# Where the four early heads are scaled in a head loop: one item sooner in VectorE's order

## What is computed

```python
def diff_core(q, k, v, q_pos, k_pos, lam):
    s = jnp.einsum('bqhjd,bkhjd->bhjqk', q, k, preferred_element_type=jnp.float32) * (DIFF_HEAD_DIM ** -0.5)
    mask = k_pos[None, :] <= q_pos[:, None]
    s = jnp.where(mask[None, None, None], s, NEG_INF)
    p = jax.nn.softmax(s, axis=-1)
    a = p[:, :, 0] - lam * p[:, :, 1]
    return jnp.einsum('bhqk,bkhe->bqhe', a.astype(v.dtype), v)
...
            o = rmsnorm(o, p['subln'][j]) * (1.0 - lam_init)
            mix = o.reshape(B, T, MIX_WIDTH)
        x = x + jnp.concatenate([mix, mem_out], axis=-1) @ p['w_out'][l]
```

## Time and profile before

| | |
|---|---|
| Median of 3 runs | 1242.99 us (1237.56, 1242.99, 1243.36) |
| The profiled execution | 1243.28 us |
| Its span | 1241.4 us |
| Mean granted clock of TensorE | 0.985 |
| TensorE busy | 1176.9 us (95%) |
| VectorE busy | 852.2 us (69%) |
| ScalarE busy | 508.5 us (41%) |
| POOL busy | 451.2 us (36%) |

### The profile page before, as it was taken

One profiled execution on the slowest core, in us unless ns is written; L12 is line 12 of the kernel. 1 busy time (PEld: TensorE's weight loads), 2 busy tenths in 40 slices (PEclk: granted clock), 3 DMA queues, 4 the chain that ended last, 5 costly groups with the idle time before them and its releaser, 6 DMA issues.

```text
span 1241.4 us, 23819 instructions
## 1 busy us (share of the span) xinstructions
PE 1176.9 (95%) x9342; PEld 1125.0 (91%) x9342; DVE 852.2 (69%) x1316; ACT 508.5 (41%) x962; POOL 451.2 (36%) x348
## 2 busy tenths in 40 slices
PE   5999898999999999999999988898999999999996
PEld 5878898999999999999899855798999999999996
DVE  6767688776776767656543787569777767767634
ACT  6545444444333433334422266434534334333321
POOL 3354035453444444212037111014544434444302
PEclk9999999999999999999999999799999999999998
DMA  7632421323223223423254277022223232232212
GB/s 273 224 128 60 142 86 52 129 76 104 101 69 119 86 73 116 148 73 102 86 157 126 87 259 258 11 86 69 86 88 116 69 116 88 69 119 86 88 49 72
DMA packets 46228, 134.95 MB, mean 109 GB/s; under 512 B 4178, under 2 KB 6354, under 8 KB 45490
## 3 DMA queue, kind: packets, MB, share of 16 engines
q1 hardware_dynamic: 45026, 125.39, 30.2%
q0 software_dynamic: 1104, 8.15, 2.2%
HBM read 123.15 MB, written 7.03 MB: 105 GB/s over the span
## 4 chain that ended last, share of the span: by engine, by line
PE 74%; DVE 12%; POOL 5%; DMA 3%; issue 3%; ACT 3%; SPq 0%; DVEq 0%; ACTq 0%; POOLq 0%
PE psum L647 29%; PE psum L629 22%; PE psum L563 15%; DVE weights_split L1420 2%; PE psum L813 1%; DVE inv_rms L1441 1%; PE psum L997 1%; DMA rotated<-projected 1%; POOL projected L2118 1%; POOL projected L2119 1%; ACT weights_split L1042 1%; DMA rotated<-keys 1%; PE psum L718 1%; DMA weights_raw<-in_weights 1%; POOL rotated L2117 1%
## 5 line engine op out<-in xcount | busy, mean ns | idle before, releaser
L647 PE MATMUL psum<-operand_b,weights_split 128*128 128x272 f32 x1536 | 197.1, 290 | 3.7 <-DVE weights_split L1509 1.9
L647 PEld LDWEIGHTS psum<-operand_b,weights_split 128*128 128x128 f32 x1536 | 195.1, 190 | 4.3 <-DVE weights_split L1509 2.2
L647 PE MATMUL psum<-operand_a,weights_split 128*128 128x272 f32 (+1 forms) x1536 | 195.3, 288 | 3.3 <-DVE weights_split L1509 1.9
L647 PEld LDWEIGHTS psum<-operand_a,weights_split 128*128 128x128 f32 x1536 | 193.5, 188 | 3.7 <-DVE weights_split L1509 2.2
L563 PE MATMUL psum<-operand_b,weights_split 128*128 128x272 f32 x1344 | 176.0, 291 | 4.4 <-DVE weights_split L1420 4.2
L563 PEld LDWEIGHTS psum<-operand_b,weights_split 128*128 128x128 f32 x1344 | 171.1, 190 | 9.3 <-DVE weights_split L1420 5.2
L563 PE MATMUL psum<-operand_a,weights_split 128*128 128x272 f32 (+1 forms) x948 | 126.7, 292 | 17.9 <-DVE weights_split L1420 13.9
L563 PEld LDWEIGHTS psum<-operand_a,weights_split 128*128 128x128 f32 x948 | 121.0, 192 | 23.9 <-issue 17.5
L1042 ACT ACTIVATE weights_split<-weights_raw 128x1024 fp32r<-128x1024 f32 (+1 forms) x66 | 66.5, 1008 | 134.2 <-PE psum L563 125.6
L1989 POOL TENSOR_TENSOR mem_keys<-weights_raw 128x512 f32<-128x512 f32 x28 | 36.7, 1312 | 219.3 <-DMA weights_raw<-in_weights 219.3
L1420 DVE TENSOR_TENSOR weights_split<-weights_raw,weights_split 128x1024 fp32r<-128x1024 f32 (+1 forms) x66 | 90.7, 1377 | 16.2 <-ACT weights_split L1042 16.1
(11 more groups left out here) (286 smaller groups left out, 2086.0 us busy)
## 6 DMA issues: line engine op xcount, KB each, us to landing
weights_raw<-in_weights SPq DMA_DIRECT2D x186, 512.0 KB, 3.7
cache_tiles<-in_page_k SPq DMA_DIRECT2D x16, 384.0 KB, 4.0
cache_tiles<-in_page_v SPq DMA_DIRECT2D x16, 384.0 KB, 4.3
cache_tiles<-in_mem_k SPq DMA_DIRECT2D x8, 512.0 KB, 4.6
cache_tiles<-in_mem_v SPq DMA_DIRECT2D x8, 512.0 KB, 5.1
residual<-in_x SPq DMA_DIRECT2D x1, 2176.0 KB, 12.0
rotated<-projected POOLq DMA_DIRECT2D x4, 408.0 KB, 7.0
rotated<-keys POOLq DMA_DIRECT2D x4, 408.0 KB, 7.1
```

Of the source, the lines that this page charges most:

```text
L647: mm = pe.matmul(ps[:, bank, 0:part.stop - part.start], w(wr), hidden[:, ar, 4 * (c % 2) + kk, part], start=(kk == 0 and wr == 0 and ar == 0),
```

## The change

The wait for sub_rms and the four scales are placed in step EARLY_DONE + 3 = 44 of VectorE's loop and no longer in step 45. There they stand behind weight(44), drain(42) and bias(46), and ahead of weight(45), drain(43) and bias(47). Nothing else is changed.

```diff
@@ -1712,7 +1712,7 @@
                     if n == EARLY_DONE + 1:
                         dve.wait_ge(squared, EARLY)
                         means(ss[:, 0:EARLY], 0, EARLY)
-                    if n == EARLY_DONE + 4:
+                    if n == EARLY_DONE + 3:
                         dve.wait_ge(sub_rms, 1)
                         for h in range(EARLY_HEADS):
                             scale_head(h)
```

## The result

The changed kernel takes 1233.68 us (median of nine runs, 1232.68 to 1238.57), the kernel before 1241.38 us in the same set (nine runs, 1237.56 to 1243.36). The ratio is 0.9945, with a 95% interval of 0.9929 to 0.9961: 0.55% faster, some 7 us. The profiled execution took 1233.68 us, its span is 1231.8.

The account below looks back on a forecast made before the run. TensorE, busy 95% of the span, was taken as the bound, waiting on VectorE's path through the scales to turn(46). Median 1242.99 less 1.3 us, clock unchanged, gave 1241.7 us; range 1236.3 to 1243.9.

Parts of the forecast that it names:

- Step 1: VectorE's scales behind bias(46): POOL's sub_rms is ready at 777.77, VectorE free at 777.96, so no wait, margin 0.19 us.
- Step 2: VectorE's order from 777.96: the scales fill its 1.38 us hole, so turn(46) starts at 784.30 instead of 785.68.
- Step 3: What becomes late: turn(45) by 1.3 us, hidden with 0.8 in hand; exp(47) by 1.02; turn(47) still gains some 1.28.
- Step 4: From turn(47) on TensorE is nearly full and transfers quiet, so everything moves up together; gain 1.3 us.
- 1.3 us: Gain on VectorE's path to turn(46) and turn(47), taken between 1.28 and 1.38 us.
- 0.06 us for POOL's clamp: First scale behind bias(46) might be held by POOL's clamp until 778.02, 0.06 later, making the gain 1.24 us.
- the term for the clock: TensorE's clock ahead of turn(46): about as thinly used after the change, so expected to fall as now; no gain counted.
- the base of 1242.99: Median of three earlier runs of the kernel before, from which the forecast subtracted its gain to reach 1241.7 us.
- Rival B: TensorE's clock never falls because its pieces lie closer together; at most 6.2 us, about 1236.5 us; chance 0.07.
- Rival A: TensorE's clock is back one step earlier because dense matmuls L997 start sooner; 1.7 us more, 1240.0 us; chance 0.25.
- C: No gain: VectorE's hole is replaced by another of the same length; 1243.0 us; chance 0.11.
- D: Slower: POOL's chain to sub_rms is late and VectorE stands in front of weight(45); 1244.4 us; chance 0.05.

Follow-up runs that it names:

- the filled kernel before: The kernel before plus eight useless TensorE matmuls, four ahead of and four behind the transposes of heads 0 and 1; 1237.85 us, ratio 0.9970.
- the pair of four matmuls: The kernel before plus four useless matmuls only ahead of the transposes of heads 0 and 1 (1241.06 us, 0.9995), or only behind them (1237.80 us, 0.9962).
- two items sooner: Scales and their wait placed behind bias(45), two items sooner than in the kernel before; 1242.63 us, ratio 1.0011.
- two more instructions: The changed kernel plus two scale-sized VectorE instructions behind bias(47), at the scales' old place; 1238.92 us, ratio 0.9986 to the kernel before.
- the fill ahead: The kernel before plus four useless TensorE matmuls only ahead of the transposes of heads 0 and 1; 1241.06 us, ratio 0.9995.

## Why the prediction was wrong

**The steps on VectorE's path held.** Step 1: the margin on sub_rms was forecast at 0.19 us and is 0.19. Step 2: turn(46) was to gain 1.38 and gained 1.46; weight(45) took 0.89 us from its start to the next instruction (778.05 to 778.94) where the sum had 0.98. Step 3: turn(47) was to gain 1.28 and gained 1.36; the wait for exp(47) appeared, 0.20 long where I had 0.1; turn(45) waits 1.12 where I had about 1.1; heads 0 and 1 start without a wait. Step 4: from there everything moved up together. (The path ahead of the fall in the kernel before did not stay wholly on TensorE, as the prediction has it: mix(47) waits 0.54 us for VectorE's drain L1675. That wait is 0.54 after the change too, and moved nothing.) The term "1.3 us" measured 1.36 to 1.37, in the profile of the changed kernel and against the filled kernel before.

**The 0.06 us for POOL's clamp** did not show: the first scale starts at 775.64, with the clamp on POOL until 775.70, and the four take 2.48 us. The bias instruction beside it was long again, 0.29 against 0.16. The same instruction in the kernel before, some 3 us earlier and beside POOL's power L2156 (773.06 to 776.00, which reads SBUF too), took 0.16:

```profile
774.60 0.16 DVE L1653 SCALAR_TENSOR_TENSOR tiny<-tiny 128x2 f32<-128x2 f32 x1
```

So the rule of the Trainium skill's page "SBUF — State Buffer" ("Who interferes with whom") agrees with the bias instruction beside the clamp, and was seen neither on the scale nor beside the power; POOL's ends are too rough to say more.

**The step that failed is the one on the clock**: "it is about as thinly used there (idle 780.3 to 781.4, pieces from 781.4 to 783.5, idle to 784.3), so I expect it to fall as now." The words were not worked out. TensorE does the same work between L843 and turn(46) in both kernels, so a turn(46) that comes 1.38 us sooner leaves it that much less idle time. In the kernel before that time is 0.50 us in front of mix(44), which the prediction overlooked, 1.47 in front of the heads and 1.59 in front of turn(46): 3.56 in all.

```profile
781.00 0.46 PE L813 MATMUL psum<-values,staging 128*128 128x128 f32 x2 [0.50 <-ACT staging L1207]
...
785.68 0.90 PE L775 MATMUL psum<-constants,probs_heads 128*128 128x128 f32 x3 [1.59 <-DVE probs_heads L1631]
```

The prediction's own list for the changed kernel comes to 1.1 and 0.8, so 1.9, and 2.07 was measured (1.12 and 0.95), with the work of turn(45), mix(44) and two heads closed up in between. "As thinly used" was thus wrong by the prediction's own numbers, and with it the term for the clock, which was put at nothing: the clock stayed at 1.00, and that is worth 5.78 us. Of the 8.0 us between the forecast and the result, this is the largest part; 1.6 are the base of 1242.99, where nine runs gave 1241.38.

That TensorE's work in this place keeps the clock up is shown by the fills (ratio 0.9970, and the stretch at 1.00). That where it stands counts too is shown by the pair of four matmuls (0.9995 and 0.9962). Rival B described what happened, for the reason it gave (TensorE's pieces lie closer together), and had 0.07; it was set aside with "a stretch of TensorE emptier, not fuller", which looked at turn(45) alone. Its size was right: 5.78 us against "6.2 us at most, some of it lost again to waits". Its time of 1236.5 was too high because it took "a microsecond of such waits", where less than half of one showed, and because the three runs of before that I had were high: 1242.99 by three, 1241.38 by nine, 1240.88 to 1241.94 in the later sets. 1241.4 less 7.15 is 1234.2, against 1233.7 and 1234.65 measured.

The timed runs agree in size without a profile. The mean granted clock of a whole execution was 0.983 to 0.989 in 21 runs of the kernel before (0.984 to 0.991 in 17 others), and 0.991 to 0.995 in the nine of the changed kernel. At half the clock, 0.006 of the mean is 0.012 of the span, some 15 us: about one low stretch. By the price of this stretch (5.78 us for 17.1, so 0.34 for each microsecond at the low clock) that is 5 us. It is an estimate: the mean counts low stretches anywhere in the execution, and the price depends on where one lies.

Rival A didn't come to be seen, since the clock did not fall. C fell with the 1.46 us. D needed sub_rms late, and it was on time; two items sooner shows what the wait looks like. The Trainium skill ("TensorE: Matmul & The Clock Gate", "What's actually happening") says that the gate follows how busy the engine has been recently, and the traces agree as far as they go: eight more matmuls brought the clock back, with no other change than the wait that they need.

**What stays open.** How much TensorE must do to keep its clock is not shown, nor why a low stretch lasted 17.1 us in three profiles of the kernel before and 3.4, 7 or 13.5 in others. Neither the length of the gap in front of turn(46) nor the sum of TensorE's idle time ahead of it orders the kernels: with two more instructions these are 2.15 and 3.27 us and the low stretch is 7 us, and with the fill ahead they are 1.59 and 2.6 and it is 13.5. Most kernels have one profile only; the kernel before has three and the changed one two. Whether the clock ever falls here in the changed kernel is not shown: neither of its two profiles has it, and the mean clocks of its 15 runs (0.989 to 0.995) don't tell where in an execution the clock was low.

## What to carry to other kernels

Where the profile shows TensorE's clock falling at the end of a thinly used stretch, price both cases before anything else is summed up: how long the low stretch is, and what its instructions take at the full clock elsewhere in the trace. A change of a microsecond on another engine's path can be worth five times that if it closes the idle time ahead of the fall, and a microsecond gained beside such a stretch can also vanish in it. Add up the engine's idle time ahead of the fall, before and after: the same work, ended 1.4 us sooner, is 1.4 us less of it. The sum alone doesn't decide, since two fills of the same size gave 0.05% and 0.38%. A fill of useless matmuls is a cheap way to tell the clock's part from the path's.

## What the runs showed of the hardware that was not expected

The clock's low stretch in the kernel before was 17.1 us in each of three profiles, and cost 5.78 us. Shorter ones cost by where they lay: one of 3.4 us over heads 2 and 3 and the first dense matmuls cost 1.34 (27.51 against 26.17 us), and one of 3.4 us over turn(46) and turn(47), where TensorE also waits for others, about 0.6. Four useless matmuls of 128x128 behind the transposes of heads 0 and 1 (1.06 us of TensorE's time) gained 0.38%, and the same four, some 2.6 us earlier in the program (1.56 and not 4.20 us after L843), gained nothing that can be told from no change (ratio 0.9977 to 1.0013). The clock also stayed up through an idle gap of 2.15 us in front of turn(46), in the changed kernel with two more instructions, and fell ahead of turn(46) in the kernel before, where the gaps are 1.47 and 1.59.
